# The inverse of a chunk and its transpose, both kept up by matmuls on four 64x64 tiles of TensorE

## The reference, cut to what matters

```python
def step(S, inp):
    r_t, w_t, k_t, v_t, a_t, b_t = inp
    sa = jnp.einsum('bhij,bhj->bhi', S, a_t)
    S = S * w_t[:, :, None, :] + sa[..., None] * b_t[:, :, None, :] + v_t[..., None] * k_t[:, :, None, :]
    y = jnp.einsum('bhij,bhj->bhi', S, r_t) if emit else None
    return S, y

S_f, y_f = rwkv_scan(states0[0], r, decay[0], k_dir[0], v, -kk, b_dir[0], False, emit)
S_b, y_b = rwkv_scan(states0[1], r, decay[1], k_dir[1], v, -kk, b_dir[1], True, emit)
```

## Time and profile before

| what | value |
|---|---|
| median of 3 runs | 2732.25 us (2727.25 to 2736.67) |
| the profiled execution | 2739.95 us, span 2738.2 us |
| TensorE: matmul running | 95% of the span |
| VectorE, ScalarE, GpSimd busy | 62%, 34%, 30% |
| stretch of jobs and steps, four pairs | 43.80, 44.60, 44.28, 44.47 us |

### The profile page before, as it was taken

How to read it: one execution, slowest core, us unless ns; L and a number is a source line. 1 busy time by engine, 2 the same in 40 slices (tenths; PEclk the granted TensorE clock), 3 DMA queues, 4 the chain that set the end, 5 groups by cost and what they waited for, 6 DMA issues and landing times. The chain is left out here.

```text
span 2738.2 us, 60351 instructions
## 1 busy us (share of the span) xinstructions
PE 2606.0 (95%) x25068; PEld 2077.8 (76%) x25068; DVE 1708.3 (62%) x3073; ACT 928.2 (34%) x2146; POOL 831.3 (30%) x1067
## 2 busy tenths in 40 slices
PE   7989999999999999999999999999999899999998
PEld 4978798795654887868688867777888677858886
DVE  5657767764525846764753358659833676577675
ACT  2013323223422225642221148321211576122571
POOL 3323344240013520012322215235531344246010
PEclk9999999999999999999999999999999999999999
DMA  6321100102432013303011152131111311122100
GB/s 235 106 95 57 45 13 9 39 15 96 156 107 91 32 62 140 125 1 108 33 62 62 62 191 68 53 115 58 36 62 62 139 63 62 62 84 93 79 3 31
DMA packets 108464, 206.05 MB, mean 75 GB/s; under 512 B 21955, under 2 KB 26194, under 8 KB 107680
## 3 DMA queue, kind: packets, MB, share of 16 engines
q1 hardware_dynamic: 107920, 201.30, 21.0%
q0 software_dynamic: 272, 0.89, 0.1%
HBM read 186.85 MB, written 15.54 MB: 74 GB/s over the span
## 5 line engine op out<-in xcount | busy, mean ns | idle before, releaser
L739 PE MATMUL psum<-weights,h_t 128*128 128x256 f32 x1488 | 355.2, 382 | 5.5 <-ACT early_work L828 5.5
L739 PEld LDWEIGHTS psum<-weights,h_t 128*128 128x128 f32 x1488 | 280.8, 191 | 45.3 <-ACT early_work L828 6.7
L739 PE MATMUL psum<-z_l,x_tiles 128*128 128x256 f32 x816 | 192.8, 379 | 0.5 <-POOL z_l L954 0.5
L1528 DVE TENSOR_REDUCE neg_max<-psum 128x1 f32<-128x768 f32 x160 | 147.1, 955 | 69.0 <-PE psum L1304 58.7
L739 PEld LDWEIGHTS psum<-z_l,x_tiles 128*128 128x128 f32 x816 | 155.0, 190 | 21.9 <-issue 0.9
L839 ACT ACTIVATE early_work<-psum 128x512 f32<-128x512 f32 (+1 forms) x80 | 45.0, 565 | 364.7 <-DVE psum L1112 248.1
L1477 ACT ACTIVATE prob<-psum,neg_max 128x768 f32<-128x768 f32 x128 | 114.1, 897 | 80.4 <-DVE neg_max L1528 80.4
L1112 DVE TENSOR_TENSOR psum<-psum,early_work 128x512 f32<-128x512 f32 x62 | 43.1, 696 | 146.3 <-PE psum L739 146.3
L1600 POOL TENSOR_TENSOR z_l<-z_l,inv_total 128x128 f32<-128x128 f32 x64 | 25.3, 400 | 310.4 <-DVE inv_total L1536 310.4
L739 PE MATMUL psum<-weights,x_tiles 128*128 128x256 f32 x496 | 117.2, 379 | 0.0
L790 PE MATMUL psum<-weights,h_t 128*128 128x512 f32 x256 | 111.5, 593 | 1.2 <-PEq L240 1.2
(11 more groups left out here) (545 smaller groups left out, 6661.2 us busy)
## 6 DMA issues: line engine op xcount, KB each, us to landing
weights<-in_ada_w_dram SPq DMA_DIRECT2D x30, 2048.0 KB, 8.2
weights<-in_a_w_in_dram SPq DMA_DIRECT2D x10, 2048.0 KB, 8.0
weights<-in_b_w_in_dram SPq DMA_DIRECT2D x8, 2048.0 KB, 8.6
weights<-in_c_w_in_dram SPq DMA_DIRECT2D x8, 2048.0 KB, 8.8
weights<-in_w_in_dram SPq DMA_DIRECT2D x6, 2048.0 KB, 8.7
x_aside<-x_tiles SPq DMA_DIRECT2D x24, 512.0 KB, 2.6
x_tiles<-x_aside SPq DMA_DIRECT2D x4, 3072.0 KB, 15.9
weights<-in_a_w_out_dram SPq DMA_DIRECT2D x4, 2048.0 KB, 7.9
```

The costliest lines, as they stand in the source:

```text
L739: last = pe.matmul(dst, lhs[:, k, :], rhs[k // 2][:, k % 2, :], start=k == 0, stop=k == KH - 1)
L1528: dve.tensor_reduce(neg_max[:, i % 4, m:m + 1], score_at(i, m), AX, ALU.max, negate=True)\
```

## The change

It replaces the jobs and the steps; the scan stays, but for two waits.

- The batches are now three, each with both directions: (8..12), (0..4), (4..8), four chunks of each direction, eight in all. There are 15 steps.
- N is made by four products for a chunk and direction: two on the diagonal tiles for N transposed, and two that write to the other half of the partitions (tiles upper right and lower left) for the plain copy `m_ab_t`, which ScalarE takes out. Head 0's copy of it, of X's left operand and of `inv` so stands on partitions 64 to 127, head 1's on 0 to 63.
- VectorE begins `inv_t` with a masked take of 512 elements and an add of the identity, both whole. `inv` is made from it by a product with the identity into the other half (`turn`), taken by ScalarE.
- In a step the first product reads the other half and writes its own (off-diagonal tiles). The second products are two: `right` (as before, 32 columns a chunk, diagonal tiles) onto `inv_t`, and `left`, `inv_t` with X into the other half, onto `inv`. The transposes on VectorE are gone. The last level has only `right`.
- The other products (`bt`, `rb`, `ak`, `kt`, `rk`, 13 fillers of 16 products) are issued between, one pair of diagonal products behind each pair of off-diagonal ones, beside the turns and the first ten first products.
- `inv` and `inv_t` get 64 columns of padding for each direction, so that one strided view covers both directions.

```diff
+            def fill(j, d, n):
+                name, bi = fillers[j]
+                left, right, _, _ = products[name]
+                cols = columns(batches[bi][0] + n)
+                for s in halves:
+                    rhs = pr.eye[s, s] if right is None else right[s, d, cols]
+                    last = pe.matmul(batch_ps(filler_bank(j))[s, d, n, :], left[s, d, cols], rhs, start=True, stop=True)
+                return last
+
+            def multiply(bi):
+                for d, n, c in pieces(bi):
+                    lhs, rhs = b["b_f"][:, d, columns(c)], b["a_f"][:, d, columns(c)]
+                    for h, s in enumerate(halves):
+                        pe.matmul(batch_ps(bi)[halves[1 - h], d, n, :], lhs[s], rhs[s], start=True, stop=True)
+                    for s in halves:
+                        last = pe.matmul(batch_ps(3 + bi)[s, d, n, :], lhs[s], rhs[s], start=True, stop=True)
                 last.then_inc(*multiplied.tick())
+            def turn(bi):
+                j = beside_turn[bi]
+                if j >= 2:
+                    pe.wait_ge(*done(j - 2))
+                pe.wait_ge(*begun.at(2 * bi + 2))
...
+                for d, n, c in pieces(bi):
+                    for h, s in enumerate(halves):
+                        last = pe.matmul(batch_ps(turned_bank(bi))[halves[1 - h], d, n, :], b["inv_t"][s, d, c, :],
+                                         pr.eye[s, s], start=True, stop=True)
+                    beside = fill(j, d, n)
...
+            def x_piece(i, d, n, c):
+                li = steps[i][0]
+                for h, s in enumerate(halves):
+                    o = halves[1 - h]
+                    last = pe.matmul(batch_ps(x_bank(i))[s, d, n, :], n_m[li % 2][o, d, c, :], b["inv"][o, d, c, :],
+                                     start=True, stop=True)
+                return last
...
+            def right_piece(i, d, n, c):
+                m = steps[i][1]
+                for s in halves:
+                    to = half_ps(right_bank(i))[s, d, n, :].rearrange("p (b m) -> p b m", m=m)
+                    last = pe.matmul(to, x_s[s, d, c, :], odd_blocks(b["inv_t"][s, d, c, :], m, d), start=True, stop=True)
                 return last
...
+            def left_piece(i, d, n, c):
+                m = steps[i][1]
+                for h, s in enumerate(halves):
+                    to = half_ps(left_bank(i))[halves[1 - h], d, n, :].rearrange("p (b m) -> p b m", m=m)
+                    last = pe.matmul(to, b["inv_t"][s, d, c, :], even_blocks(x_s[s, d, c, :], m, d), start=True, stop=True)
+                return last
...
+            for bi in range(3):
+                multiply(bi)
+            turn(0)
+            turn(1)
+            first_product(0)
+            turn(2)
+            first_product(1)
+            for i in range(2, final + 1):
+                second_products(i - 2)
+                first_product(i)
+            second_products(final - 1)
+            first_product(final + 1)
+            last_product(final, x=final + 2)
+            last_product(final + 1)
+            last_product(final + 2)
...
+            def begin(bi):
+                a, e = batches[bi]
+                t = b["inv_t"][:, :, a:e, :]
+                dve.wait_ge(*multiplied.at(bi + 1))
+                dve.tensor_tensor(t, batch_ps(3 + bi), both("up1"), ALU.mult).then_inc(*begun.tick())
+                dve.wait_ge(*begun.at(2 * bi + 1))
+                dve.tensor_tensor(t, t, wide(wide(eye, 1, e - a), 1, 2), ALU.add).then_inc(*begun.tick())
...
+            def add(i):
+                _, m, bi = steps[i]
+                a, e = batches[bi]
                 dve.wait_ge(*p_done.at(i + 1))
+                if i < final:
+                    t = left_blocks(b, m, a, e)
+                    products = half_ps(left_bank(i)).rearrange("p d c (b m) -> p d (c b) m", m=m)
+                    dve.tensor_tensor(t, t, products, ALU.add).then_inc(*added.tick())
+                t = right_blocks(b, m, a, e)
+                products = half_ps(right_bank(i)).rearrange("p d c (b m) -> p d (c b) m", m=m)
                 dve.tensor_tensor(t, t, products, ALU.add).then_inc(*added.tick())
-                if li < final:
-                    dve.wait_ge(*added.at(i + 1))
-                    dve.transpose(b["inv"][:, d, a:e, :], b["inv_t"][:, d, a:e, :]).then_inc(*mirrored.tick())
...
+            def take_turned(bi):
+                a, e = batches[bi]
+                act.wait_ge(*turned.at(bi + 1))
+                act.activation(b["inv"][:, :, a:e, :], batch_ps(turned_bank(bi)), ACT.Copy).then_inc(*turned_out.tick())
+                take(beside_turn[bi])
```

More of the change, by code:

```diff
@@ L3722, in rwkv_core_stage @@
     s_decayed = pr.counter("sc_s_decayed")
[L3723 to L3733, removed]
@@ L3751, in rwkv_core_stage @@
[L3751 to L3755, removed]
+    batches = [(XC, NC), (0, XC // 2), (XC // 2, XC)]
+    steps = [(li, m, bi) for li, m in enumerate(LEVELS[1:]) for bi in range(3)]
+    final = 3 * (len(LEVELS) - 2)
+    products = dict(rb=(b["b_f"], b["r_f"], "up_i", b["m_rb"]), rk=(b["k_f"], b["r_f"], "up_i", b["m_rk"]),
+                    ak=(b["k_f"], b["a_f"], "up", b["m_ak"]), bt=(b["b_f"], None, None, b["b_tok"]),
+                    kt=(b["k_f"], None, None, b["k_tok"]))
@@ new lines, in rwkv_core_stage, with both @@
+    fillers = [("bt", 0), ("bt", 1), ("rb", 1), ("bt", 2), ("rb", 2), ("ak", 0), ("ak", 1), ("ak", 2),
+               ("kt", 0), ("kt", 1), ("kt", 2), ("rk", 1), ("rk", 2)]
+    beside_turn, beside_x = {0: 0, 1: 1, 2: 3}, {0: 2, 1: 4, **{i: i + 3 for i in range(2, 10)}}
+    with_b = 5
+    v_order = [j for j, (name, _) in enumerate(fillers) if products[name][2]]
+    a_order = [j for j, (name, _) in enumerate(fillers) if not products[name][2]]
+    eye = masks[:, MASKS.index("eye"), :]
+    def both(name):
+        x = MASKS.index(name)
+        return wide(masks[:, x:x + 2, :], 2, 4)
@@ L3783, in rwkv_core_stage @@
         W, S, Y, U = 0, 2, 4, 6
-        X, B = 6, 4
         @block.tensor
         def _(pe):
[L3788 to L3798, removed]
-                last.then_inc(*multiplied.tick())
-            def products(bank, lhs, rhs, i, half=None):
-                li, m, bi = steps[i]
[L3803 to L3814, removed]
-                return last
-            def finish(i):
-                li, m, bi = steps[i]
-                d = batches[bi][0]
@@ new lines, in pieces, with columns @@
+            def pieces(bi):
+                a, e = batches[bi]
+                return [(d, n, a + n) for d in range(2) for n in range(e - a)]
+            def columns(c):
+                return slice(col_of(c), col_of(c) + CH)
+            def fill(j, d, n):
+                name, bi = fillers[j]
+                left, right, _, _ = products[name]
[4 more added lines that the diff above has]
+                return last
@@ new lines, in first_product @@
+            def first_product(i):
+                wait_x(i)
+                j = beside_x.get(i)
+                if j is not None:
+                    pe.wait_ge(*done(j - 2))
+                for d, n, c in pieces(steps[i][2]):
+                    last = x_piece(i, d, n, c)
+                    if j is not None:
+                        beside = fill(j, d, n)
+                last.then_inc(*x_done.tick())
+                if j is not None:
+                    beside.then_inc(*filled.tick())
@@ L3825, in finish @@
[L3825 to L3840, removed]
@@ L3966, in take_w @@
+            for bi in range(3):
+                begin(bi)
+            for j in (2, 4):
+                take(j)
+            for i in range(len(steps)):
+                add(i)
+                j = beside_x.get(i + 2)
+                if j in v_order:
+                    take(j)
             def take_w(n, d):
```

209 lines of the change are left out of this document (121 added, 88 removed).

## The result

The changed kernel takes 2798.01 us (median of 4 runs, 2794.68 to 2799.34) against 2734.46 for the kernel before in the same session: ratio 1.0235, 95% interval 1.0212 to 1.0258. It is slower by 64 us, where I had forecast 37 less. That is the rival of no overlap by its number (2803), but not by its picture, as the profile shows.

A forecast was written before the change was run, and what follows sets the result against it. TensorE's own order of work was taken to bound four stretches of 177.15 us in all. 32.6 + 2.4 + 0.15 = 35.1 us per pair, 140.4 for four, 36.7 less: 2695.5 us, 8-in-10 range 2684 to 2733.

The forecast's parts named there:

- the rival of no overlap: Rewritten stretches: groups of four products go as 64 blocks, 62.1 us per pair of heads, 2803 us; chance 0.17.
- the change part by part: Rewritten stretches: 1024 products for 736, but in 35 blocks for 46, 32.6 us per pair of heads for 42.8.
- Overlap of four quadrants: Blocks of 32 products: four tiles run at once, a group taking the 117 ns of a pair; chance 0.66.
- The rival that two tiles on the same rows take turns: Second form of no overlap in the new groups of four: they go as two pairs, 2803 us; chance 0.06.
- the half overlap: Groups of four: only two neighbours share passes, 137 ns a group, 19 us more in all, 2714 us; chance 0.12.
- the one for full overlap: Sign in the changed trace: records 15 ns apart in blocks of 32 products, 64 records in 0.93 us.
- its first form, the feed: TensorE is fed at most one record each 29 ns, so four tiles gain nothing, 2803 us; chance 0.11.
- Its break-even: The change loses once a group of four takes 157 ns, 9.2 us being won over 232 groups.
- The start of the stretch: First eight blocks: VectorE's identity adds wait beside GpSimd, TensorE stalls 2.4 us, against some 1.0 without the collision.
- The steady part: Steps of two blocks, 1.86 us: other engines need 1.51 us at most, hidden with 1.0 to 1.2 us slack.
- Another engine becomes the bound: Steps: VectorE's adds take 0.75 us, not 0.42, so TensorE waits, 10 us in all, 2706 us; chance 0.05.
- the clock: TensorE is granted full speed in nearly every slice, so its clock was given no part in the sum.

The follow-up runs named there:

- the narrow groups: Kernel before plus 512 products of 64 columns in groups of four tiles at the start of each core stage: 2851.54 us, ratio 1.0426.
- Extra pairs: Kernel before plus idle off-diagonal product pairs ahead of the diagonal first products of levels 4 to 32, results thrown away: 2781.47 us, ratio 1.0179.
- the wide groups: Kernel before plus 128 products of 256 columns in groups of four tiles at the start of each core stage: 2790.91 us, ratio 1.0210.
- the fillers apart: Changed kernel with each block of filler products issued behind its turn or first product, not pair by pair between: 2797.01 us.

## Why the prediction was wrong

**The step that failed** is in the change part by part: "If a group of four takes the 117 ns that a pair takes now, this is 35 blocks, 35 x 0.93 = 32.6 us. I take that value". The group does take 117 ns, once its instructions are there. The term that I left out is that they are not: 4096 instructions at the 14.1 ns that the narrow groups show are 58 us of the 59.9 measured, whatever the tiles do. I had posed the right question, "the price of one tile's passes ... or of feeding TensorE with instructions?", and then answered the first half of it only. All the neighbours of the earlier trace rows have at least 59 ns for a load and a matmul, so none of them could test the feed; the one row that could, one record each 29 ns, was the same for 32 columns and for 64, and I read that as a floor of the tile. It is both: tile and supply ask for nearly the same pace in the kernel before, 58 ns for a pair's pass and 14 to 15 ns for an instruction. Extra pairs that cost no tile time cost 63 ns a product there, which shows the second.

**Overlap of four quadrants: right.** It had been argued from rows and columns apart; the wide groups show it (55 ns a record of 256 columns), and the changed kernel's own timeline (14.6 ns a record of 64). The rival that two tiles on the same rows take turns is out, and so is the half overlap. Of the signs that I had set down, the one for full overlap (records 15 ns apart) and one against it (TensorE idle) came true together, the idleness between lots of instructions and not in front of each block.

**The rival of no overlap: right in size, 2803 against 2798, and its first form, the feed, is the cause.** I gave it 0.11 and its evidence ("no row shows a quicker rate over a block") was the stronger evidence. That the number came out is in part luck: my price for it, 64 x 0.93, was a pace of blocks on the tiles, and it equals the pace of supply because the two happen to lie so close. Its break-even, 40 ns more for a group of four, was passed: a group of four products is 16 instructions, and 16 x 14.6 = 234 ns stand against 157.

**The start of the stretch: right, and without effect.** Predicted were batches begun 3.7, 5.5 and 7.4 us after the first product, because VectorE's add with two inputs in SBUF waits for GpSimd. The trace has them at 3.7, 5.4 and 7.1:

```profile
226.27 1.78 DVE L4061 TENSOR_TENSOR rwkv_work<-rwkv_work,masks 128x512 f32<-128x512 f32 x1
...
228.68 1.05 DVE L4061 TENSOR_TENSOR rwkv_work<-rwkv_work,masks 128x512 f32<-128x512 f32 x1
...
230.37 1.06 DVE L4061 TENSOR_TENSOR rwkv_work<-rwkv_work,masks 128x512 f32<-128x512 f32 x1
```

(226.27 + 1.78 - 224.33 = 3.72.) The 2.4 us of stall a pair that I drew from it, 9.6 in all, do not show: in front of the turns TensorE waited 1.5 us for these adds over the four stretches, and of all its stillness in the first stretch only 0.2 us was for another engine. They fall into pauses of the supply.

**The steady part: durations right, their cover moot.** The left and right adds take 0.42 each, X 0.60, GpSimd's masks 1.28, as taken. VectorE, ScalarE and GpSimd wait for TensorE, TensorE almost never for them. "Another engine becomes the bound" is out.

**What I had held out of the sum: the clock.** I wrote that it is no part of the story. It became a small part: the granted clock is 0.89 to 0.94 in the stretches and 0.88 in the first scan, and the scans are 1.2 us longer each, some 5 us in all. With the fillers apart, too, the scan took 25.5 us where the clock was 1.00 and 26.8 where it was 0.88. What brings the clock down is open. Standing still alone did not: without its left products TensorE was idle for 28% of the first stretch (35.26 of 49.02 us busy) at a granted clock of 1.00, and in the narrow groups of the first stage for 36% (18.60 of 29.00 us busy), also at 1.00. In the stretches the lower clock costs nothing that the runs show: the run with the fillers apart had 1.00 in its first and took 62.31 us.

## What to carry to other kernels

Count TensorE's instructions as well as its columns. In this kernel long unbroken runs of small fp32 matmuls, each of four instructions, were paid by the instruction, 14.1 to 15.1 ns each, and tiles that run side by side did not pass that. A stretch in which a profile shows spells of 256 instructions and pauses named "issue" is at that limit. Before packing tiles in such a place, divide the stretch by its instructions, and if it comes out near 15 ns, take instructions away (fewer, wider matmuls, which no run here tried on the kernel's own products) or leave it. And where evidence for a rate comes only from slower neighbours, a change that doubles the rate has not been tested by them.

## What the runs showed of the hardware that I had not expected

- Instructions come to TensorE in packets of 16 KB, 256 instructions, one each 3.45 or 4.0 us in the narrow groups, 3.3 to 4.4 between full lots of the changed kernel, when it is short of them: 14.1 ns an instruction with nothing else going on. Of a lot of 3.45 us the packet itself takes 1.1. What sets the rest, and why some lots take 4.0, is open: nothing here varied the packets or their queue, and no such run was tried.
- At the start of a stage more is at hand: the changed kernel and the narrow groups both work off 366 matmuls and loads within 3.0 us before their first pause.
- Four tiles of 64x64 run at once at 58 ns for four matmul records and their four loads, in spells of 256 instructions.
- The kernel before already took 15.3 ns an instruction in these stretches, and its tiles and its supply ask for nearly the same time, which is why packing tiles gained nothing. Moving products away is another matter: it did shorten the stretch (by 3.3 us with kt and rk), and the scan that took them in gave most of it back (2.8).
